# Routing on column strips, slab splits moved ahead of it, and the last expert's rows added by a selection matrix

## What is computed

```python
logits = h @ w_router + b_router                      # 264 x 8
top_v, top_i = top_k(logits, 2); gates = softmax(top_v)
for e in range(8):                                    # w1, w3: 1024 x 3584, w2: 3584 x 1024
    out += gate[:, e] * ((silu(h @ w1[e]) * (h @ w3[e])) @ w2[e])
y = x + gt * rms_norm(out, g_post_ffn)
```

## Time and profile before

| | |
|---|---|
| median of three runs | 1728.03 us |
| the profiled execution | 1726.33 us, span 1724.5 us |
| PE busy | 1586.0 us (92%) |
| DVE busy | 1247.3 us (72%) |
| ACT busy | 981.1 us (57%) |
| DMA | 513.05 MB, mean 298 GB/s |
| mean granted TensorE clock | 0.953 of 2.4 GHz |

### The profile page before, as it was taken

One profiled execution on the slowest core, in us unless ns is written; L12 is line 12 of the kernel. 1 busy time (PEld: TensorE's weight loads), 2 busy tenths in 40 slices (PEclk: granted clock), 3 DMA queues, 4 the chain that ended last, 5 costly groups with the idle time before them and its releaser, 6 DMA issues.

```text
span 1724.5 us, 22944 instructions
## 1 busy us (share of the span) xinstructions
PE 1586.0 (92%) x8712; PEld 1303.2 (76%) x8712; DVE 1247.3 (72%) x1088; ACT 981.1 (57%) x881; POOL 141.3 (8%) x133
## 2 busy tenths in 40 slices
PE   6889999799898678699999999999999999999991
PEld 3579999598785455488888888888888888888881
DVE  4455543668783533578888888888888888889884
ACT  2244432433232432377777777877877777777771
POOL 0000000025531421100000000000000000000001
PEclk9799999899899879699999999999999999999996
DMA  9895544945568127589999999999999999999972
GB/s 344 303 337 180 180 159 152 343 143 201 166 226 312 59 68 287 206 316 374 374 390 378 355 395 382 363 388 372 381 384 366 382 387 354 395 378 370 383 275 89
DMA packets 248396, 513.05 MB, mean 298 GB/s; under 512 B 8999, under 2 KB 68567, under 8 KB 248319
## 3 DMA queue, kind: packets, MB, share of 16 engines
q1 hardware_dynamic: 241015, 490.27, 79.2%
q0 software_dynamic: 4912, 17.67, 2.7%
q10 hardware_dynamic: 2400, 4.17, 0.7%
HBM read 498.19 MB, written 14.35 MB: 297 GB/s over the span
## 4 chain that ended last, share of the span: by engine, by line
PE 79%; DVE 9%; DMA 4%; POOL 3%; ACT 2%; issue 2%; POOLq 0%; ACTq 0%; DVEq 0%
PE wide L466 23%; PE wide L467 22%; PE wide L468 22%; POOL phase L1830 2%; DVE phase L1523 2%; PE wide L517 1%; DMA ring<-in_ada_ffn_w 1%; PE wide L528 1%; PE wide L901 1%; DVE w_lo L1753 1%; POOL phase L1836 1%; PE wide L503 1%; DMA ring<-in_cache_v 1%; ACT w_hi L1236 1%; DMA ring<-in_ada_mix_w 1%
## 5 line engine op out<-in xcount | busy, mean ns | idle before, releaser
L1753 DVE TENSOR_TENSOR w_lo<-ring,w_hi 128x2048 fp32r<-128x2048 f32 x336 | 768.3, 2291 | 116.0 <-ACT w_hi L1236 114.6
L1236 ACT ACTIVATE w_hi<-ring 128x2048 fp32r<-128x2048 f32 x336 | 643.3, 1919 | 212.6 <-PE wide L468 212.5
L466 PE MATMUL wide<-w_hi,xe_hi 128*128 128x512 f32 x896 | 355.7, 397 | 5.9 <-DVE xe_lo L1758 4.1
L468 PE MATMUL wide<-w_hi,xe_lo 128*128 128x512 f32 x896 | 350.3, 391 | 0.0
L467 PE MATMUL wide<-w_lo,xe_hi 128*128 128x512 f32 x896 | 349.7, 390 | 0.0
L396 DVE TENSOR_TENSOR w_lo<-ring,w_hi 128x2048 fp32r<-128x2048 f32 (+1 forms) x58 | 139.1, 2401 | 111.1 <-ACT w_hi L965 110.8
L466 PE MATMUL wide<-tHi,w_hi 128*128 128x264 f32 x672 | 198.6, 295 | 20.4 <-DVE mLo L1441 20.4
L467 PE MATMUL wide<-mLo,w_hi 128*128 128x264 f32 x736 | 212.7, 289 | 0.0
L466 PEld LDWEIGHTS wide<-w_hi,xe_hi 128*128 128x128 f32 x896 | 168.8, 188 | 43.8 <-DVE w_lo L1753 6.2
L468 PEld LDWEIGHTS wide<-w_hi,xe_lo 128*128 128x128 f32 x896 | 168.5, 188 | 35.9
L467 PEld LDWEIGHTS wide<-w_lo,xe_hi 128*128 128x128 f32 x896 | 169.0, 189 | 33.3
(11 more groups left out here) (286 smaller groups left out, 1696.7 us busy)
## 6 DMA issues: line engine op xcount, KB each, us to landing
ring<-in_moe_w SPq DMA_DIRECT2D x336, 1024.0 KB, 6.9
ring<-in_ffn_w SPq DMA_DIRECT2D x30, 1024.0 KB, 5.4
ring<-in_ada_mix_w SPq DMA_DIRECT2D x24, 1024.0 KB, 8.6
ring<-in_ada_ffn_w SPq DMA_DIRECT2D x24, 1024.0 KB, 12.0
ring<-in_w_q SPq DMA_DIRECT2D x12, 1024.0 KB, 9.4
ring<-in_cache_k SPq DMA_DIRECT2D x24, 512.0 KB, 5.0
ring<-in_cache_v SPq DMA_DIRECT2D x24, 512.0 KB, 6.6
ring<-in_w_kv SPq DMA_DIRECT2D x8, 1024.0 KB, 6.4
```

The source lines that it names most:

```text
L466: pe.matmul(out, a[0], b[0], start=start, stop=False, skip_group_check=True)
L468: return pe.matmul(out, a[1], b[0], start=False, stop=stop, skip_group_check=True)
L1236: act.activation(w_hi[:, (NSPLIT + k) % PAIRS, :], ring[:, slot, :], ACT.Copy).then_inc(hi_done, 1)
L1753: dve.tensor_tensor(w_lo[:, i, :], ring[:, slot, :], w_hi[:, i, :].bitcast(F32), ALU.subtract).then_inc(lo_done, 1)
```

## The change

On TensorE the logits are now formed with the experts on partitions: four matmuls write four column strips of 32 (router weights spread to 32 columns in `c32` by ScalarE), over all 264 tokens at once, for each half of `hT`. VectorE adds the bias while it evicts them to `std`, and three matmuls with `fold` sum the strips and turn them to token rows. The turns of `hT` are put between these steps. The split of expert 0's first three slabs stands ahead: ScalarE's three copies before the evictions of `hT`, VectorE's first remainder after the ranking, the other two after the row numbers. The sum of each expert's load goes to its own semaphore.

At the end, the last expert's rows are not stored. While it runs, GpSimd gathers the other experts' rows of one token tile at a time (zeroed first, since rows of expert 7 are left out by the bound), and VectorE adds them with their gates at slabs 14, 20 and 26 (`early_sum`). A selection matrix `pickT` (slot by token, holding the gate) is built during the routing; after expert 7 TensorE multiplies `ye` by it and VectorE adds the result to the sum. ScalarE loads its table for the square root before it waits for that.

```diff
+            def logit_strips(hf):
+                pe.wait_ge(rw_spread, 1)
+                pe.wait_ge(h_ready, 7 + hf)
+                for i in range(4):
+                    mm = pe.matmul(bank[1][32 * i:32 * (i + 1), 0:NT], c32[:, 4 * hf + i, :], hT[:, 4 * hf + i, :], start=(hf == 0), stop=(hf == 1))
+                mm.then_inc(lg_strips, 1)
...
+            logit_strips(0)
+            token_rows(0)
+            token_rows(1)
+            logit_strips(1)
+            token_rows(2)
+            pe.wait_ge(lg_evicted, 1)
+            for c, n in ((0, P), (1, P), (2, NB)):
+                mm = pe.matmul(bank[0][0:n, NE * c:NE * (c + 1)], std[:, P * c:P * c + n], fold[:, 0:NE], start=True, stop=True)
+            mm.then_inc(lg_summed, 1)
...
+            pe.wait_ge(ht_taken, KC)
+            pe.matmul(bank[2][:, 0:P], ones, before, start=True, stop=True).then_inc(count_row, 1)
             pe.wait_ge(gate_rows, 1)
...
+            pe.wait_ge(pick_ready, 1)
+            for q, n in enumerate(rows):
+                mm = pe.transpose(bank[2][:, P * (q + 1):P * (q + 1) + n], pick[0:n, q, :], ident[0:n, 0:n])
+            mm.then_inc(pick_turned, 1)
             pe.wait_ge(gate_taken, 1)
             pe.wait_ge(moe_ready, 1)
...
             experts(0)
+            pe.wait_ge(pick_taken, 1)
+            pe.wait_ge(y0_copied, NE + 1)
+            pe.wait_ge(y1_copied, NE + 1)
+            for q, n in enumerate(rows):
+                for h in range(2):
+                    mm = pe.matmul(wide[q][0:n, 512 * h:512 * (h + 1)], pickT[:, P * q:P * q + n], ye[:, 512 * h:512 * (h + 1)], start=True, stop=True)
+                mm.then_inc(merged, 1)
...
+            act.activation(c32[:, :, 0:NE], rw[:, :, :], ACT.Copy)
+            act.activation(c32[:, :, NE:NE + 1], c32[:, :, NE + 1:NE + 2], ACT.Copy).then_inc(rw_spread, 1)
...
+            act.wait_ge(pick_turned, 1)
+            act.activation(pickT, bank[2][:, P:P + NT], ACT.Copy).then_inc(pick_taken, 1)
...
+            dve.wait_ge(lg_strips, 2)
+            dve.tensor_scalar(std[:, :], bank[1][:, 0:NT], rb_strip, None, ALU.add).then_inc(lg_evicted, 1)
...
+            for q, n in enumerate(rows):
+                ins = dve.tensor_scalar(pick[0:n, q, :], bank[2][0:n, 0:P], r_a[0:n, q, 1, NE - 1:NE], gate[0:n, q, NE - 1:NE], ALU.is_equal, ALU.mult)
+            ins.then_inc(pick_ready, 1)
...
+            def early_sum(q):
+                n = rows[q]
+                dve.wait_ge(early_in, 32 * (q + 1))
+                link(dve.tensor_scalar(early[0][0:n, :], early[0][0:n, :], gpair[0:n, 0, q:q + 1], None, ALU.mult))
+                dve.scalar_tensor_tensor(part[q][0:n, :], early[1][0:n, :], gpair[0:n, 1, q:q + 1], early[0][0:n, :], ALU.mult, ALU.add)\
+                   .then_inc(early_done, 1)
...
                 for k, (m, j, half) in enumerate(eslabs):
+                    if last and c == 0 and k in (14, 20, 26):
+                        early_sum((k - 14) // 6)
...
             experts(0)
+            tiles = tuple(enumerate((P, P, NB)))
+            dve.wait_ge(early_done, 3)
+            for q, n in tiles:
+                dve.wait_ge(merged, q + 1)
+                dve.tensor_tensor(part[q][0:n, :], part[q][0:n, :], wide[q][0:n, :], ALU.add).then_inc(f_ready, 1)
             overflow = dve.value_load(flag[0:1, 0:1], min_val=0, max_val=1)
...
+            def collect_early():
+                for q, n in enumerate(rows):
+                    if q:
+                        pool.wait_ge(early_done, q)
+                    pool.memset(hflat[0:n, 0:2 * D], 0.0).then_inc(early_zero, 1)
+                    pool.wait_ge(early_zero, q + 1)
+                    for i in range(2):
+                        pool.indirect_dma_start(early[i][0:n, :], None, y_rows[0][0:EARLY_ROWS, :],
+                                                bass.IndirectOffsetOnAxis(ap=row[0:n, 0, i, q:q + 1], axis=0),
+                                                bounds_check=EARLY_ROWS - 1, oob_is_err=False).then_inc(early_in, 16)
+                pool.wait_ge(early_done, 3)
```

More of the change, by code:

```diff
@@ L38 @@
 ROWS = (NE * SLOTS, (PASSES - 1) * NE * SLOTS)
+EARLY_ROWS = (NE - 1) * SLOTS
 NEG = -1e30
@@ L822, in _, with token_rows @@
             ada_columns(3, 5)
[L825 to L833, removed]
+            def logit_strips(hf):
[4 more added lines that the diff above has]
+                mm.then_inc(lg_strips, 1)
+            def token_rows(k):
                 if k >= 2:
@@ L838, in _ @@
                 mm.then_inc(ht_turned, 1)
+            logit_strips(0)
[7 more added lines that the diff above has]
+            mm.then_inc(lg_summed, 1)
+            for k in range(3, 7):
+                token_rows(k)
             pe.wait_ge(sel_ready, 1)
@@ L1271, in experts @@
             def experts(c):
-                for k in range(PAIRS):
-                    high(0, c, k)
+                if c:
+                    for k in range(PAIRS):
+                        expert_high(0, c, k)
                 gathered_high(0, c, 0)
@@ L1717, in _ @@
             dve.tensor_scalar(row[:, 1], r_d, -float(ROWS[0]), None, ALU.add).then_inc(row_ready, 1)
+            for k in range(1, PAIRS):
+                expert_low(0, 0, k)
             dve.wait_ge(lg_exp, 1)
@@ L1788, in experts @@
             def experts(c):
-                for k in range(PAIRS):
-                    low(0, c, k)
+                if c:
+                    for k in range(PAIRS):
+                        expert_low(0, c, k)
                 gathered_low(0, c, 0)
@@ L1800, in _ @@
                     experts(c)
-            tiles = tuple(enumerate((P, P, NB)))
-            for q, n in tiles:
-                dve.wait_ge(y_back[q], 32)
-                link(dve.tensor_scalar(back[0:n, q, :], back[0:n, q, :], gpair[0:n, 0, q:q + 1], None, ALU.mult))
-                dve.scalar_tensor_tensor(fout[0:n, q, :], back[0:n, 3 + q, :], gpair[0:n, 1, q:q + 1], back[0:n, q, :], ALU.mult, ALU.add)\
-                   .then_inc(f_ready, 1)
+                dve.wait_ge(f_ready, 3)
+                dve.wait_ge(y_over, 16 * 6)
+                for i in range(2):
+                    for q, n in tiles:
+                        ins = dve.scalar_tensor_tensor(part[q][0:n, :], back[0:n, 3 * i + q, :], gpair[0:n, i, q:q + 1], part[q][0:n, :], ALU.mult, ALU.add)
+                    ins.then_inc(over_added, 1)
+                    dve.wait_ge(over_added, i + 1)
             for q, n in tiles:
@@ L1900, in experts @@
                         rows_in(e + 1, c)
+                    if done == NE - 1:
+                        pool.wait_ge(xe_turned, 2 * NE)
+                        collect_early()
+                        pool.wait_ge(merged, 3)
+                        pool.sem_inc(y_free, 1)
+                        continue
                     pool.wait_ge(y0_copied, done + 2)
```

108 lines of the change are left out of this document (65 added, 43 removed).

## The result

Five runs of the changed kernel gave a median of 1714.03 us (1712.1 to 1717.48), five of the kernel before on the same chip 1729.29 (1725.89 to 1732.83): 0.9915 of the time before, 95% interval 0.99 to 0.993. In a second batch six runs gave 1711.93 (1709.57 to 1715.54), ratio 0.9914 (0.9898 to 0.993). The forecast was 1707.0: the direction and the sign of each of the three terms were right, the gain was 15 us where 20 were announced, and the time lies 1 us above the range. The profiled execution took 1712.1 us, its span is 1709.9.

What follows compares the result with a forecast made beforehand. TensorE bounds the experts, but not the routing or the last 35.2 us. Terms -6.8 + 2.3 - 15.9 = -20.4 from a mean of 1727.4 gave 1707.0 us, range 1701 to 1713.

Steps and rivals of the forecast that it cites:

- the three terms: Routing up to the first expert matmul minus 6.8 us, last expert plus 2.3, end minus 15.9.
- Logits and row numbers: Routing: logits ready at 697.4, a gain of 6.1 us; row numbers at 704.6 against 713.3 before.
- Scattered rows: GpSimd's scatters and read of expert 0's rows unchanged at 14.0 us, ending at 718.6; slabs 7 to 9 charged nothing.
- Gates: Routing, VectorE's longer chain: spread 6.0 us, evictions ending at 721.9, then 4.6 to the first expert matmul at 726.5.
- The first sign that I gave for being wrong: Routing: the forecast is wrong if the scattered rows come last; it had them at 718.6, before the spread's evictions at 721.9.
- The last expert: Last expert: three TensorE stalls of 0.5 us, 1.6 in all, and 0.7 for zeroing; plus 2.3 (0 to 4.4).
- The zeroing: Last expert: GpSimd's zeroing slows VectorE's remainders by 0 to 1.4 us, taken as 0.7; by the skill's rule 0.
- The end: After the last expert matmul: end at T+19.3 instead of T+35.2, minus 15.9 us (17.3 without the flag).
- the jump: End: VectorE's branch over the overflow passes costs 0.5 us, after 0.9 for loading the flag.
- the fetch: Rival at the end: VectorE's final jump waits for its code by DMA, 3.5 us more, 1710.5; chance 0.12.
- the last sign for being wrong: End: the forecast is wrong if VectorE stands still after the last addition for more than 2 us.
- the cases: Whole kernel: forecast 0.60, all short (1702) 0.13, fetch (1710.5) 0.12, cold TensorE (1714.4) 0.07, late gathers 0.05, nothing 0.03.

Runs made afterwards that it cites:

- e1: Changed kernel with VectorE's remainders 1 to 3 of the first expert moved behind the copy of the gates: one profile, 1713.51 us.
- e2: Changed kernel with slabs 7 to 9 requested only once expert 0's rows have been read: one profile, 1711.8 us.
- e8: Changed kernel with the last expert's rows taken back, routing alone kept: median 1724.2 us, 0.9981 of the kernel before; A, second strips to first expert matmul, 34.98.
- e4: Changed kernel with VectorE's flag load and branch ahead of the three merged additions, which stand in both arms: 1710.11 us.
- e3: Changed kernel without the overflow pass, its flag loads and branches on every engine: 1711.98 us, last copy to end of span 17.67 instead of 21.49.
- e6: Changed kernel with each early sum split, its scaling two slabs ahead of the rest: 1709.99 us.
- e7: Changed kernel with early sums split, flag and branch ahead of additions, remainders 1 to 3 behind gates' copy: median 1702.35 us, 0.9865 of the kernel before.

## Why the forecast was right in kind and wrong in size

**Logits and row numbers: right.** Forecast 697.4 and 704.6; measured 697.47 and 704.52. The first half of the hidden state was 0.7 earlier, so the chain to the logits took 0.7 longer than I had it, half of it in the longer pause between the halves.

**Scattered rows: the step that failed first.** The forecast carried 14.0 us over "unchanged" from the row numbers to the turn and charged nothing for slabs 7 to 9, because "they end before the last scatter". It took 20.5 (704.52 to 725.00). Two things were missed. The remainders that the change puts right behind the row numbers stand beside GpSimd's first scatters and cost 2.4 us there (2.65 + 1.83 instead of 1.05 + 0.99; e1 removes it). And the slabs that these remainders set free were in the queues when the last scatter came: 4.1 us (6.14 of idle instead of 2.03; e1 and e2 remove it). Together they are the 6.5. But only the last 1.9 of it set the time (evictions at 723.1, turn at 725.0), and less, some 0.6, in executions with a colder TensorE (e1, e2).

**Gates: the second part of the miss.** Evictions at 723.1, forecast 721.9: the spread ran at a granted clock of 0.50 from 714.9 on and took 7.1 us (713.46 to 720.57), where I took 6.0 between 4.1 and 8.2. From the turn to the first expert matmul it was 4.6, as forecast. So the 3.8 that the routing lacks are 0.7 ahead of the logits, 1.2 in the spread and 1.9 in the rows. These are shares of one chain and not prices: in e8 the spread was as short as forecast, and the rows alone kept A at 34.98. The first sign that I gave for being wrong, that the scattered rows come last, came true.

**The last expert: right.** 2.8 against 2.3. The sums stalled TensorE three times by about 0.67 (0.78 between starts before the first, 0.34 behind it, where 0.23 is the pace), 2.0 in all instead of 1.6. The zeroing cost 0 instead of 0.7, as the rule of the Trainium skill on "SBUF: two separate sides" ("SBUF — State Buffer") had it: the trace agrees, 6.69 us for three remainders beside it. The 0.8 that remains is the first expert, which ran at half the clock for 4.9 us instead of 3.1.

```profile
729.62:734.48 4.86, 4.86 (x12) 3.84 (x13) 0.00 (x0) 0.00 (x0) 0.00 (x0) 0.50 0.14 57
```

(Columns: TensorE's matmuls and weight loads, VectorE, ScalarE, GpSimd, granted clock, DMA share, GB/s.)

**The end: the step that failed by size.** 13.7 instead of 15.9 less. Evictions, merge, additions and the finals (10.2) were within 0.2. I took 0.9 us for the flag from a row of GpSimd and added 0.5 for the jump, for which I had no row, with the fetch as a rival of 0.12. The jump costs 2.97 us (e4), the flag ahead of it some 0.3, and both are worth 3.8 (e3). So the rival's price came true, with 2.5 more where it had 3.5, and so did the last sign for being wrong, VectorE still for more than 2 us. In all the stillness was 3.71 instead of 1.4: this 2.3 is the whole miss of the end. The row of GpSimd was the wrong neighbour: its next instruction came 0.43 behind the branch, and why its own jump was so much cheaper than VectorE's no run shows. What the Trainium skill says in "Instruction fetch mechanics" ("Runtime: NRT & Kernel Launch"), that a taken branch beyond the loaded pages waits for a fetch by DMA, fits the three packets of the instruction queue in the gap; it is not shown that the branch waited for them.

**The sum.** The profile lacks 5.8 of the 20.4: 3.1 in the routing (3.8 less the front's 0.7), 0.5 in the experts, 2.2 at the end. The fetch alone was a case inside the range (1710.5); I weighed the cases as alternatives, and several held at once, which put the time at 1714.

## What to carry to other kernels

Where work is pulled ahead into an idle gap, ask what the neighbours do in the same microseconds: here two harmless remainders slowed GpSimd's indirect DMAs and released transfers into the queues of the one that mattered. The branch over a long piece of code that is hardly ever run cost VectorE about 3 us where nothing covered it; load its flag and take it while another engine works, and put the dependent instructions behind it. When the front of a kernel varies by 6 us between executions, measure edits by the stretch in which they act.

## What the runs showed of the hardware

- GpSimd's indirect DMAs took 2.65 and 1.83 us to issue beside VectorE's subtractions of two SBUF operands, and 1.05 and 0.99 without them (e1). VectorE itself lost nothing (4.49 us for two), and a zeroing by GpSimd in the same place took 1.82 and did not disturb VectorE.
- The last scatter, with slabs in flight, landed in 6.73 us (714.31 to 721.04), and in 2.5 with the slabs held (e2); GpSimd's wait for it was 6.14 and 1.94.
- A jump over the unused pass took VectorE 2.97 us (e4), and ScalarE stood still 2.66 at the same place. With flag and jump behind the last addition VectorE's whole stillness was 3.69 to 3.83 us in four profiles and 2.67 in e6, so the price varies by about 1 us.
- One of GpSimd's gathers took 4.84 us to issue (e7), where its like took 2.63 in the changed kernel.
